# Where two of four RWKV pairs get their gates: behind the input projection, or between the levels of a triangular solve

## The chip, the cores and the metric

The kernel runs on one core of a Trainium2 chip. The metric is the device time of one launch in microseconds (us). Five engines work side by side and wait for each other by semaphores: TensorE (PE in the profile; PEld is its weight load), VectorE (DVE), ScalarE (ACT), GpSimd (POOL) and SyncE (SP), which here only issues DMAs. Each takes its instructions strictly in the order in which the program lists them.

## The reference, cut to what matters

One decoder layer for 512 prompt tokens and 8 sampled tokens (520 columns in all): a SwiGLU block, an input projection that feeds a differential-attention group and an RWKV-7 group, an output projection, and a second SwiGLU block. The change touches the RWKV part alone:

```
xm = prw + (prev - prw) * mu                      # token shift of the projected rows
r, k, v, xw, xa, xg = split(xm)                   # 512, 512, 512, 64, 64, 128 columns
w_log = -softplus(-(w0 + tanh(xw) @ w2)) - 0.5
decay = exp(-exp(w_log))                          # = exp(-exp(-0.5) * sigmoid(w0 + tanh(xw) @ w2))
a     = sigmoid(a0 + xa @ a2)
kk    = k * k_k;  kk = kk / max(sqrt(sum over a head of kk*kk), 1e-12)
k     = k * (1 + (a - 1) * k_a);   b = kk * a
# per head, over the tokens:  S = S * decay + (S @ -kk) b^T + v k^T ;  o = S @ r
```

The 8 RWKV heads of 64 are handled as 4 pairs of 128 rows (pairs 0 to 3). "Lora products" are `tanh(xw) @ w2` and `xa @ a2`; the two sigmoids of them are the decay gate and the rate gate.

## The kernel before

Everything lies feature-major: 128 partitions by 520 columns. The order of the whole program is written out by hand, one list of steps for each engine.

**Input projection** (`input_tensor`, `input_scalar`, `input_vector`, `input_pool`). 26 slabs j = 0..25, each one chunk of 128 output features, 48 matmuls. The order of chunks is RWKV's small columns (24, 25: tanh(xw) and xa, xg), the rotary chunks, then keys, r and v of the pairs and the attention values. Slabs from 4 on use accumulators 0 and 1 in turn; accumulator 2 is free for small products, and accumulator 3 takes the cache logits. Behind slab j (in order on TensorE) come the small steps: lora halves of pair 0 behind slabs 12 and 14, of pair 1 behind 18 and 20 (`half_lora_tensor`, two matmuls each), head sums of the squared keys behind 15 and 21 (`summed_tensor`), and from slab 10 on one group of cache pages each (`decode_keys_tensor`, 8 matmul records). ScalarE splits the next weights, drains the slab and does the gates; VectorE does the low halves of the split weights, the token shift and the exponents.

**Phase 0/1** then handles pairs 0 and 1 on the engines: an opening (`opening_tensor`, products and transposes of the features), five levels l = 0..4 that double the size of inverted blocks (`levels_tensor`, `levels_scalar`, `levels_vector`), a solve, and a state chain over n = 1..7 (`chain_tensor`, `chain_vector`). Within each level two ticks of attention are woven in (tick 2l + n): logits, maximum on VectorE, two exponentials with sums on ScalarE, a scaling, a transposition; and groups of cache pages. **Phase 2/3** does the same for the other pairs. Pairs 2 and 3 get their gates in phase 0/1: at level 0 (pair 2) and level 3 (pair 3) TensorE makes both lora products (`lora_tensor`, L964/L965), ScalarE the two sigmoids (`gates_scalar`, L1012/L1013) into the scratch rows LW and AG, the key factor and the squared keys (`factor_scalar`, L1022, L1024); at levels 1 and 4 TensorE sums the squares per head (L979), ScalarE takes the root (L1972), and VectorE the reciprocal behind level 1 and in the solve (`keys_inverse_vector`, L1075/L1076). VectorE's scans (L1057) and POOL's exponents and products follow, and POOL ends a pair with two copies into the step columns (L1121/L1122), on which the next pair's gates wait.

**PSUM ring.** The small products of the phases go through four banks in a fixed order (`ring_order`): a job may start when the jobs that held its banks have been read. The lora products are two jobs of two banks, that is the whole ring, and the key sums one job of one bank.

**State chain.** For every n, TensorE multiplies the states (L1844) and VectorE adds (L2272); step n + 1 waits for both. In phase 0/1 VectorE does after n = 4: `step_out_vector` (L2136, L2141), `decode_sums_vector` (seven small operations, L1387 to L1393) and `bonus_terms_vector` (L2147). TensorE's `decode_weights_tensor` (L1409) at n = 5 waits for the decode sums.

SP issues weight and page loads; the load of the third lora matrix (LG2, same space as LORA) waits for pair 3's rate product.

Of the kernel before, what the change touches and what calls it, by code (L numbers as in the profile page):

```python
# [112 lines left out]
def layer(nc, x_in, gu_a, down_a, w_in, w_out, gu_b, down_b, consts, vecs, lams, lora, g2,  # L113
# [15 lines left out]
    lo_dram = nc.dram_tensor("trunk_lo", (P, DC, TOK), f32, kind="Internal").ap()  # L129

    ctx = ExitStack()
    with ctx:
# [658 lines left out]
        def ring_order():  # L791
# [10 lines left out]
            for two, before, nxt in (((0, 1), (), (2, 3)), ((2, 3), (0, 1), ())):  # L802
# [14 lines left out]
                for l in range(N_LEVELS):  # L817
# [4 lines left out]
                    if nxt and l in (0, 3):  # L822
                        add(("decay", nxt[l // 3]), "s", 2)
                        add(("rate", nxt[l // 3]), "s", 2)
                    if nxt and l in (1, 4):
                        add(("keys", nxt[l // 4]), "s")
# [133 lines left out]
        def lora_tensor(pe, i, w, a):  # L960

            for n in range(2):
                cols = slice(HALF * n, HALF * n + HALF)
                m0 = nc.tensor.matmul(w[:, n, 0:HALF], LORA[0:64, i, :], PROJ[0:64, 24, cols], start=True, stop=True)  # L964
                m1 = nc.tensor.matmul(a[:, n, 0:HALF], LORA[64:P, i, :], PROJ[64:P, 24, cols], start=True, stop=True)  # L965
            return m0, m1
# [31 lines left out]

        def decay_gate_scalar(act, i):
            act.wait_ge(g("lora_done"), 2 * i + 1)  # L1000
            if i:
                act.wait_ge(g("step_columns"), i)
            nc.scalar.activation(halves(LW), accv(2), ACT.Sigmoid, bias=pv(i, 0)).then_inc(g("decay_read"), 1)

        def rate_gate_scalar(act, i):
            act.wait_ge(g("lora_done"), 2 * i + 2)
            nc.scalar.activation(halves(AG), accv(2), ACT.Sigmoid, bias=pv(i, 1)).then_inc(g("rate_read"), 1)

        def gates_scalar(act, i, w, a):

            act.wait_ge(g("step_columns"), i)
            nc.scalar.activation(halves(LW), w, ACT.Sigmoid, bias=pv(i, 0)).then_inc(g("bank_read_s"), 1)  # L1012
            nc.scalar.activation(halves(AG), a, ACT.Sigmoid, bias=pv(i, 1)).then_inc(g("bank_read_s"), 1)  # L1013

        def factor_scalar(act, i):
# [3 lines left out]
            else:  # L1019
                was_taken(act, ("rate", i))  # L1020
            act.wait_ge(g("vectors_set"), 1)
            nc.scalar.activation(FACTOR[:, :], AG, ACT.Identity, scale=pv(i, 3), bias=KEPT_KA[:, i:i + 1]).then_inc(g("gates"), 1)  # L1022
            was_shifted(act, 16 + i)
            nc.scalar.activation(KN, pj(16 + i), ACT.Square, scale=pv(i, 2)).then_inc(g("keys_squared"), 1)  # L1024
# [47 lines left out]
        def keys_inverse_vector(dve, i):  # L1072

            was_taken(dve, ("keys", i))
            dve_then(dve, nc.vector.tensor_scalar(KN[:, 0:HALF], KN[:, 0:HALF], 1e-12, None, ALU.max))  # L1075
# [159 lines left out]
        def input_scalar(act):  # L1235
            for j in range(N_IN):
# [22 lines left out]
                if j == 21:  # L1259
                    decode_own_scalar(act)  # L1260
# [1462 lines left out]
```

## Time and profile before

| | |
|---|---|
| three runs, us | 1325.09, 1330.69, 1326.98 (median 1326.98) |
| the profiled execution | 1320.13 us, its span 1318.3 us |
| granted TensorE clock, mean | 0.986 |
| PE busy | 1253.5 us (95%) |
| DVE busy | 558.8 us (42%) |
| ACT busy | 425.7 us (32%) |
| POOL busy | 109.1 us (8%) |
| chain that ended last | PE 84%, DVE 6%, ACT 3%, issue 2%, SPq 2%, DMA 1% |

Times inside the execution count from the start of its span. The first SwiGLU block ends at about 400 us, the input projection runs to 589 us, phase 0/1 to 735 us, phase 2/3 to 850 us, and the rest is output projection, second SwiGLU block and norms. A time in brackets in a timeline row is how long the engine was idle before the instruction and who released it. PEclk is the granted share of the full clock of 2.4 GHz: 0.50 is 1.2 GHz.

### The profile page before, as it was taken

How to read it: one execution, taken by the hardware profiler on the slowest of the kernel's cores; microseconds unless marked ns; L12 is line 12 of the kernel's file. 1: busy time of each engine (PE TensorE's matmuls, PEld its weight loads, DVE VectorE, ACT ScalarE, POOL GpSimd, SP SyncE). 2: the span in 40 equal slices, each digit the busy share in tenths (PEclk: the TensorE clock that was granted, in tenths of full speed). 3: DMA queues.
4: the chain of work that ended last, by engine and by line, in shares of the span. 5: the costliest groups of instructions: out<-in, count | busy, mean ns of one | idle time of the engine just before them, and what ended most of it. 6: DMA issues, size and time to landing. Idle time of an engine off the chain costs nothing.

```text
span 1318.3 us, 30092 instructions
## 1 busy us (share of the span) xinstructions
PE 1253.5 (95%) x12902; PEld 1132.4 (86%) x12902; DVE 558.8 (42%) x818; ACT 425.7 (32%) x657; POOL 109.1 (8%) x101
## 2 busy tenths in 40 slices
PE   9999999999998999997887999898999999999996
PEld 7999999999998988875446545697999999999995
DVE  4323332323436444253563554668533332322253
ACT  4222223221323324324553334323422222221222
POOL 0000000000110110000450012013000000000021
PEclk9999999999999999998998999999999999999999
DMA  6222222222223667544453799751222222222221
GB/s 226 96 95 92 75 88 95 68 89 88 88 86 112 260 198 248 193 154 146 157 165 119 246 312 313 251 186 35 94 96 95 95 95 93 67 79 88 89 65 66
DMA packets 56692, 174.79 MB, mean 133 GB/s; under 512 B 7185, under 2 KB 7442, under 8 KB 48274
## 3 DMA queue, kind: packets, MB, share of 16 engines
q1 hardware_dynamic: 54578, 169.48, 38.4%
q10 hardware_dynamic: 2016, 3.88, 0.8%
q8 instruction: 75, 1.23, 0.4%
q14 instruction: 23, 0.19, 0.0%
HBM read 163.58 MB, written 9.76 MB: 131 GB/s over the span
## 4 chain that ended last, share of the span: by engine, by line
PE 84%; DVE 6%; ACT 3%; issue 2%; SPq 2%; DMA 1%; POOL 0%; ACTq 0%; DVEq 0%
PE acc L295 66%; PE acc L318 5%; PE acc L1362 2%; SPq L2457 1%; PE acc L1432 1%; PE acc L971 1%; PE acc L1627 1%; PE acc L1619 1%; SPq L2449 1%; PE acc L1594 1%; PE acc L1604 1%; DVE weights_lo L278 1%; ACT map L1554 1%; PE acc L1510 1%; DMA y_sum<-in_x 1%
## 5 line engine op out<-in xcount | busy, mean ns | idle before, releaser
L278 DVE TENSOR_TENSOR weights_lo<-weights_raw,weights_hi 128x1024 fp32r<-128x1024 f32 (+2 forms) x184 | 208.4, 1134 | 533.4 <-ACT weights_hi L271 533.3
L271 ACT ACTIVATE weights_hi<-weights_raw 128x1024 fp32r<-128x1024 f32 (+2 forms) x184 | 177.5, 967 | 551.8 <-PE acc L295 520.8
L295 PE MATMUL acc<-x_hi,weights_hi 128*128 128x260 f32 x1696 | 344.2, 284 | 1.2 <-DVE weights_lo L263 1.2
L295 PE MATMUL acc<-x_hi,weights_lo 128*128 128x260 f32 x1696 | 341.7, 283 | 0.0
L295 PE MATMUL acc<-x_lo,weights_hi 128*128 128x260 f32 x1696 | 341.1, 283 | 0.0
L295 PEld LDWEIGHTS acc<-x_hi,weights_hi 128*128 128x128 f32 x1696 | 261.7, 188 | 14.3 <-issue 11.7
L295 PEld LDWEIGHTS acc<-x_hi,weights_lo 128*128 128x128 f32 x1696 | 261.4, 188 | 0.0
L295 PEld LDWEIGHTS acc<-x_lo,weights_hi 128*128 128x128 f32 x1696 | 260.7, 188 | 0.0
L295 PE MATMUL acc<-hidden_hi,weights_hi 128*128 128x260 f32 x704 | 143.1, 284 | 0.0
L295 PE MATMUL acc<-hidden_hi,weights_lo 128*128 128x260 f32 x704 | 141.7, 283 | 0.0
L295 PE MATMUL acc<-hidden_lo,weights_hi 128*128 128x260 f32 x704 | 141.6, 283 | 0.0
L295 PEld LDWEIGHTS acc<-hidden_hi,weights_hi 128*128 128x128 f32 x704 | 108.5, 188 | 1.7 <-issue 1.6
L295 PEld LDWEIGHTS acc<-hidden_lo,weights_hi 128*128 128x128 f32 x704 | 108.6, 188 | 0.0
L295 PEld LDWEIGHTS acc<-hidden_hi,weights_lo 128*128 128x128 f32 x704 | 108.6, 189 | 0.0
L593 POOL TENSOR_TENSOR scratch<-y_sum 128x520 f32<-128x520 f32 x3 | 4.8, 1613 | 664.2 <-DVE y_sum L372 664.2
L345 ACT ACTIVATE hidden_hi<-scratch 128x520 f32 (+1 forms) x44 | 28.1, 639 | 85.8 <-DVE scratch L355 85.8
L358 DVE TENSOR_TENSOR hidden_lo<-scratch,hidden_hi 128x520 f32 (+1 forms) x44 | 30.8, 701 | 38.9 <-ACT hidden_hi L345 38.9
L1362 PE MATMUL acc<-cache_pages,query_columns 128*32 128x512 f32 x256 | 35.8, 633 | 0.0
L318 PE MATMUL acc<-x_hi,weights_hi 128*128 128x260 f32 x128 | 26.5, 289 | 6.8 <-DVE x_lo L688 6.8
L1604 PEld LDWEIGHTS acc<-level_y,inverse_turned 64*64 64x64 f32 x768 | 13.8, 137 | 20.3 <-issue 16.9
L599 POOL TENSOR_TENSOR scratch<-scratch,y_sum 128x520 f32<-128x520 f32 x15 | 25.0, 1666 | 70.8 <-DVE y_sum L436 66.9
L355 DVE TENSOR_TENSOR scratch<-scratch,acc 128x520 f32<-128x520 f32 x44 | 30.3, 689 | 0.0
(337 smaller groups left out, 1338.3 us busy)
## 6 DMA issues: line engine op xcount, KB each, us to landing
cache_pages<-in_cache_k SPq DMA_DIRECT2D x128, 256.0 KB, 3.5
weights_raw<-in_gate_up_b SPq DMA_DIRECT2D x22, 1024.0 KB, 4.8
weights_raw<-in_gate_up_a SPq DMA_DIRECT2D x21, 1024.0 KB, 4.8
cache_pages<-in_cache_v SPq DMA_DIRECT2D x64, 256.0 KB, 3.7
weights_raw<-in_w_in SPq DMA_DIRECT2D x13, 1024.0 KB, 6.4
projected<-in_cache_v SPq DMA_DIRECT2D x48, 256.0 KB, 3.6
weights_raw<-in_down_a SPq DMA_DIRECT2D x8, 768.0 KB, 4.2
weights_raw<-in_down_b SPq DMA_DIRECT2D x8, 768.0 KB, 4.2
```

Of the source, the lines that this page charges most:

```text
L271: nc.scalar.activation(WH[pr.slot(k)][:, 0:nk, :], RAW[slot][:, 0:nk, P * (k % 2):P * (k % 2) + P], ACT.Copy).then_inc(split_hi, 1)
L278: nc.vector.tensor_tensor(WL[pr.slot(k)][:, 0:nk, :], RAW[slot][:, 0:nk, P * (k % 2):P * (k % 2) + P], WH[pr.slot(k)][:, 0:nk, :].bitcast( ...
L295: mm = nc.tensor.matmul(acc[s][:, a, 0:HALF], w[slot][:, t, :], x[:, k0 + t, HALF * a:HALF * a + HALF], start=begins and t == tiles[0] and ...
L318: mm = nc.tensor.matmul(acc[s][:, a, 0:HALF], w[slot][:, t, :], x[:, t, HALF * a:HALF * a + HALF], start=seen[k] == 1 and m == 0, stop=see ...
L345: nc.scalar.activation(HH[:, bass.ds(2 * (i - 1) + k - 2, 1), :], SCR[:, k:k + 1, :], ACT.Copy).then_inc(h_hi, 1)
L355: dve.tensor_tensor(halves(SCR[:, k, :]), halves(SCR[:, k - 2, :]), accv(k), ALU.mult).then_inc(hidden, 1)
L358: dve.tensor_tensor(HL[:, bass.ds(c, 1), :], SCR[:, k:k + 1, :], HH[:, bass.ds(c, 1), :].bitcast(f32), ALU.subtract).then_inc(acc_free[k], 1)
L599: pool.tensor_tensor(SCR[:, 5, :], Y[:, 0, :] if c == 1 else SCR[:, 5, :], Y[:, c, :], ALU.add)\
L971: mm = nc.tensor.matmul(out[:, n, 0:HALF], weights, x[:, HALF * n:HALF * n + HALF], start=True, stop=True)
L1362: mm = nc.tensor.matmul(bank(DECODE_BANK)[32 * h:32 * h + 32, :], QZ[:, h, b, :], PG[k % RING_GROUPS][:, :, P * h:P * h + P], start=b == 0 ...
L1432: mm = nc.tensor.matmul(bank(DECODE_BANK)[32 * j:32 * j + 8, :], WZ[:, n, 8 * b:8 * b + 8], page(N_GROUPS + k, j), start=False, stop=k == ...
L1604: mm = nc.tensor.matmul(two_banks(name)[64 * q:64 * q + 64, r, 64 * k:64 * k + 64], flat(lhs)[rows, cols], flat(rhs)[rows, cols], start=Tr ...
```

## The change

The lora halves of all four pairs are computed behind slabs 12, 13, 14, 16, 17, 18, 19 and 20 of the input projection, through accumulator 2. The gates of pairs 2 and 3 are put into rows 0, 1, 4, 5 of Y and written to a DRAM tensor by ScalarE's queue (behind slabs 15, 17, 18, 20); the squared keys of pairs 2 and 3 follow into rows 4 and 5, one folded sum behind slab 24, one root, and one reciprocal for both pairs at slab 25, kept in Y row 1. In levels 0 and 3 ScalarE issues two DMAs that bring the gates back into LW and AG and makes the key factor behind the exponentials of the level's first tick. The ring loses its lora and key jobs. In the state chain the decode sums (phase 0/1) and the bonus terms (both phases) move from n = 4 to n = 5 on VectorE. Decay gates of pairs 0 and 1 move one slab forward on ScalarE.

```diff
+        HALF_AT = {12: (0, 0), 13: (2, 0), 14: (0, 1), 16: (2, 1), 17: (3, 0), 18: (1, 0), 19: (3, 1), 20: (1, 1)}
+        HALF_ORDER = list(HALF_AT.values())
+        EARLY = [half for half in HALF_ORDER if half[0] >= 2]
+        EARLY_ROWS = (0, 1, 4, 5)
+        KEYS_INVERSE = Y[:, 1, 0:HALF]
+        def half_free(pe, j):
...
+            if j in (13, 19):
+                pe.wait_ge(g("decay_read"), j // 19 + 1)
+            if j in (14, 17, 18, 20):
+                pe.wait_ge(g("early_gates"), {14: 1, 17: 2, 18: 3, 20: 4}[j])
+            if j == 16:
+                pe.wait_ge(g("keys_normed"), 1)
+        def early_gate_scalar(act, half):
+            n = EARLY.index(half)
+            half_done(act, half)
+            act.wait_ge(g("roped"), 8)
+            nc.scalar.activation(halves(Y[:, EARLY_ROWS[n], :]), accv(2), ACT.Sigmoid, bias=pv(*half)).then_inc(g("early_gates"), 1)
+        def early_gate_out(act, n):
+            act.wait_ge(g("early_gates"), n + 1)
+            act.dma_start(gates_dram[n, :, :], Y[:, EARLY_ROWS[n], :]).then_inc(g("early_saved"), 16)
+        def early_squares_scalar(act, i):
+            act.wait_ge(g("early_saved"), 4 * 16)
+            was_shifted(act, 16 + i)
+            nc.scalar.activation(Y[:, 2 + i, :], pj(16 + i), ACT.Square, scale=pv(i, 2)).then_inc(g("early_squares"), 1)
+        def early_keys_tensor(pe):
+            pe.wait_ge(g("keys_normed"), 2)
+            pe.wait_ge(g("early_squares"), 2)
+            folded_tensor(acc[2][:, 0, :], (Y[:, 4, :], Y[:, 5, :])).then_inc(g("early_summed"), 1)
+        def early_keys_scalar(act):
+            act.wait_ge(g("early_summed"), 1)
+            nc.scalar.activation(KEYS_INVERSE, acc[2][:, 0, 0:HALF], ACT.Sqrt).then_inc(g("early_normed"), 1)
+        def early_keys_vector(dve):
+            dve.wait_ge(g("early_normed"), 1)
+            dve_then(dve, nc.vector.tensor_scalar(KEYS_INVERSE, KEYS_INVERSE, 1e-12, None, ALU.max))
+            nc.vector.reciprocal(KEYS_INVERSE, KEYS_INVERSE).then_inc(g("keys_inverse"), 1)
+        def gates_back(act, i):
+            act.wait_ge(g("step_columns"), i)
+            act.wait_ge(g("early_saved"), 4 * 16)
+            for n, x in enumerate((LW, AG)):
+                act.dma_start(x, gates_dram[2 * i - 4 + n, :, :]).then_inc(g("gates_back"), 16)
...
@@ input_scalar: per slab j
-                if j in (13, 19):
-                    decay_gate_scalar(act, j // 19)
+                if j in (12, 18):
+                    decay_gate_scalar(act, j // 18)
+                if j in (15, 17, 18, 20):
+                    early_gate_out(act, (15, 17, 18, 20).index(j))
+                if j in (13, 17, 19):
+                    early_gate_scalar(act, HALF_AT[j])
+                if j in (22, 23):
+                    early_squares_scalar(act, j - 20)
+                if j == 24:
+                    early_keys_scalar(act)
...
                 if j in (16, 22):
                     decays_scalar(act, j // 22)
+                if j == 16:
+                    early_gate_scalar(act, HALF_AT[j])
@@ input_vector
+                if j == 25:
+                    early_keys_vector(dve)
@@ levels_tensor
-                if nxt and l in (0, 3):
-                    i = nxt[l // 3]
-                    ring_free(pe, ("decay", i))
-                    ring_free(pe, ("rate", i))
-                    for mm in lora_tensor(pe, i, two_banks(("decay", i)), two_banks(("rate", i))):
-                        ring_full(mm)
-                if nxt and l in (1, 4):
...
-                    ring_full(folded_tensor(one(("keys", i)), (KN, KN)))
@@ levels_scalar
                 if nxt and l in (0, 3):
-                    i = nxt[l // 3]
-                    take(act, ("decay", i))
-                    take(act, ("rate", i))
-                    gates_scalar(act, i, wide(("decay", i)), wide(("rate", i)))
-                    factor_scalar(act, i)
-                if nxt and l in (1, 4):
...
-                    was_read(nc.scalar.activation(KN[:, 0:HALF], one(("keys", i))[:, 0:HALF], ACT.Sqrt), ("keys", i))
+                    gates_back(act, nxt[l // 3])
...
                 for n in range(2):
                     attention_exp_scalar(act, 2 * l + n, a, b)
+                    if nxt and l in (0, 3) and n == 0:
+                        factor_scalar(act, nxt[l // 3])
                     attention_turn_scalar(act, 2 * l + n, a, b)
@@ levels_vector, solve_vector
-                    if nxt and 2 * l + n == 3:
-                        keys_inverse_vector(dve, nxt[0])
...
-            if nxt:
-                keys_inverse_vector(dve, nxt[1])
@@ chain_vector
                 if n == 4:
                     step_out_vector(dve, b)
-                    if nxt:
-                        decode_sums_vector(dve)
-                    bonus_terms_vector(dve, b)
+                if nxt and n == 5:
+                    decode_sums_vector(dve)
                 if nxt and n >= 5:
                     for name in OPENED_AT[n]:
                         opened_vector(dve, name)
+                if n == 5:
+                    bonus_terms_vector(dve, b)
@@ sync, page group 28
-                    full(sp, ("rate", 3))
+                    sp.wait_ge(g("lora_done"), len(HALF_ORDER))
```

## Rows read from the trace of the kernel before

**Rows 1.** Windows, input projection: us, engines' busy, PEclk, DMA share, GB/s.
```profile
470.00:590.00 120.00, 119.06 (x985) 100.98 (x984) 52.40 (x107) 40.75 (x68) 5.85 (x8) 1.00 0.59 194
```

**Rows 2.** Chain of waits, a half product: start us, us, what.
```profile
490.09 1.07 PE acc L995 x4
```

**Rows 3.** Timeline of VectorE, opening of phase 0/1: start, duration, [idle before].
```profile
590.81 0.69 DVE L2152 TENSOR_TENSOR t_turned<-acc,constants 128x512 f32<-128x512 f32 x1 [0.88 <-PE acc L1594]
```

**Rows 4.** Timeline of TensorE, opening and level 0.
```profile
591.64 1.29 PE L1594 MATMUL acc<-features 64*64 64x64 f32 x64 [0.53 <-DVE t_turned L2152]
...
619.29 1.11 PE L1524 MATMUL acc<-projected 64*128 64x256 f32 x4 [2.26 <-ACT map L1554]
```

**Rows 5.** Timeline of ScalarE, level 0.
```profile
610.15 0.60 ACT L1920 ACTIVATE inverse_turned<-acc 128x512 f32<-128x512 f32 x1 [0.22 <-PE acc L1627]
...
613.07 1.28 ACT L1012 ACT_TABLE_LOAD   x1 [2.33 <-PE acc L965]
...
615.68 0.82 ACT L1022 ACTIVATE y_sum<-scratch,kept_key,feature_vectors 128x520 f32<-128x520 f32 x1
...
617.14 1.28 ACT L1554 ACT_TABLE_LOAD   x1
...
621.50 0.47 ACT L1554 ACTIVATE map<-acc,prompt_small 128x256 f32<-128x256 f32 x1 [1.37 <-DVE prompt_small L1568]
```

**Rows 6.** Timeline of VectorE, level 0: maximum of the first logits.
```profile
613.79 0.43 DVE L1568 TENSOR_REDUCE prompt_small<-acc 128x2 f32<-128x256 f32 x1 [4.34 <-PE acc L1527]
```

**Rows 7.** Windows of 2 us: TensorE's granted clock in stretches of 2 and 12 us.
```profile
618.00:620.00 2.00, 0.71 (x4) 0.39 (x4) 0.38 (x2) 1.99 (x7) 0.00 (x0) 0.86 0.81 237
...
640.00:642.00 2.00, 1.97 (x36) 1.88 (x37) 1.26 (x3) 0.00 (x0) 1.92 (x2) 0.50 0.05 12
...
694.00:696.00 2.00, 0.26 (x16) 0.12 (x8) 0.00 (x0) 0.00 (x0) 0.00 (x0) 1.00 0.68 201
...
715.00:727.00 12.00, 11.69 (x116) 9.52 (x119) 2.52 (x7) 1.42 (x3) 0.00 (x0) 0.50 0.12 43
```

**Rows 8.** Timeline of ScalarE, first exponentials of levels 1, 3 and 4.
```profile
630.62 0.58 ACT L1554 ACTIVATE map<-acc,prompt_small 128x384 f32<-128x384 f32 x1
...
661.06 0.47 ACT L1554 ACTIVATE map<-acc,prompt_small 128x256 f32<-128x256 f32 x1
...
670.69 0.58 ACT L1554 ACTIVATE map<-acc,prompt_small 128x384 f32<-128x384 f32 x1
```

**Rows 9.** Timeline of VectorE, levels 1 and 4.
```profile
628.60 0.96 DVE L1568 TENSOR_REDUCE prompt_small<-acc 128x2 f32<-128x768 f32 x1 [1.84 <-PE acc L1527]
...
636.97 1.78 DVE L1076 RECIPROCAL scratch<-scratch 128x260 f32<-128x260 f32 x1
...
668.67 0.96 DVE L1568 TENSOR_REDUCE prompt_small<-acc 128x2 f32<-128x768 f32 x1 [1.24 <-PE acc L1527]
```

**Rows 10.** Timeline of TensorE, level 1.
```profile
626.85 0.65 PE L979 MATMUL acc<-scratch,constants 128*32 128x260 f32 x8
...
640.03 1.13 PE L1604 MATMUL acc<-inverse,t_turned 64*64 64x64 f32 x32 [2.34 <-DVE value_blocks L2130]
```

**Rows 11.** Timeline of POOL: last copy of pair 2's features.
```profile
654.03 0.20 POOL L1122 COPY step_columns<-scratch 128x8 f32<-128x8 f32 x1
```

**Rows 12.** Landing times: tile decode_state, then the cache pages' issues.
```profile
DMA to landing us min/median/max: 2.0/5.8/11.0
...
cache_pages<-in_cache_k SPq DMA_DIRECT2D x128, 256.0 KB, 3.5
```

**Rows 13.** Timeline of VectorE, state chain at n = 4.
```profile
710.46 0.69 DVE L2141 TENSOR_REDUCE group_out<-value_blocks 128x8 f32<-128x512 f32 x1
...
713.27 0.47 DVE L2272 SCALAR_TENSOR_TENSOR state_added<-acc,gains,state_added 128x64 f32<-128x64 f32 x2
```

**Rows 14.** Timeline of TensorE, state chain at n = 5.
```profile
713.70 0.69 PE L1594 MATMUL acc<-features 64*64 64x64 f32 x32 [2.16 <-DVE state_added L2272]
...
714.32 3.06 PE L1409 MATMUL acc<-weight_columns,y_sum 128*128 128x64 f32 x16
```

More of the change, by code:

```diff
@@ L129, in layer @@
     lo_dram = nc.dram_tensor("trunk_lo", (P, DC, TOK), f32, kind="Internal").ap()
+    gates_dram = nc.dram_tensor("early_gates", (4, P, TOK), f32, kind="Internal").ap()
     ctx = ExitStack()
@@ L958, in layer @@
         KAPPA = math.exp(-0.5)
[L960 to L966, printed above, removed]
         def summed_tensor(out, weights, x):
@@ L997, in half_lora_tensor, with half_done @@
             mm.then_inc(g("lora_done"), 1)
+        HALF_AT = {12: (0, 0), 13: (2, 0), 14: (0, 1), 16: (2, 1), 17: (3, 0), 18: (1, 0), 19: (3, 1), 20: (1, 1)}
[3 more added lines that the diff above has]
+        KEYS_INVERSE = Y[:, 1, 0:HALF]
+        def half_done(eng, half):
+            eng.wait_ge(g("lora_done"), HALF_ORDER.index(half) + 1)
+        def half_free(pe, j):
+            if j == 12:
+                pe.wait_ge(g("rope_sin"), 8)
+                pe.wait_ge(g("lora_in"), 16)
+                pe.wait_ge(g("rates_in"), 1)
+            if j in (13, 19):
[4 more added lines that the diff above has]
+                pe.wait_ge(g("keys_normed"), 1)
@@ L1005, in rate_gate_scalar @@
         def rate_gate_scalar(act, i):
-            act.wait_ge(g("lora_done"), 2 * i + 2)
+            half_done(act, (i, 1))
             nc.scalar.activation(halves(AG), accv(2), ACT.Sigmoid, bias=pv(i, 1)).then_inc(g("rate_read"), 1)
[L1009 to L1013, printed above, removed]
         def factor_scalar(act, i):
@@ L1019, in factor_scalar @@
             else:
-                was_taken(act, ("rate", i))
+                act.wait_ge(g("gates_back"), 32 * (i - 1))
             act.wait_ge(g("vectors_set"), 1)
             nc.scalar.activation(FACTOR[:, :], AG, ACT.Identity, scale=pv(i, 3), bias=KEPT_KA[:, i:i + 1]).then_inc(g("gates"), 1)
-            was_shifted(act, 16 + i)
-            nc.scalar.activation(KN, pj(16 + i), ACT.Square, scale=pv(i, 2)).then_inc(g("keys_squared"), 1)
+            if i < 2:
+                was_shifted(act, 16 + i)
+                nc.scalar.activation(KN, pj(16 + i), ACT.Square, scale=pv(i, 2)).then_inc(g("keys_squared"), 1)
         def decays_scalar(act, i):
@@ L1963, in levels_scalar @@
                 if nxt and l in (0, 3):
-                    i = nxt[l // 3]
-                    take(act, ("decay", i))
-                    take(act, ("rate", i))
-                    gates_scalar(act, i, wide(("decay", i)), wide(("rate", i)))
-                    factor_scalar(act, i)
-                if nxt and l in (1, 4):
-                    i = nxt[l // 4]
-                    take(act, ("keys", i))
-                    was_read(nc.scalar.activation(KN[:, 0:HALF], one(("keys", i))[:, 0:HALF], ACT.Sqrt), ("keys", i))
+                    gates_back(act, nxt[l // 3])
                 if nxt and l == 2:
```

34 lines of the change are left out of this document (9 added, 25 removed).

## The prediction

> **What bounds the kernel now.** I read the windows first. In the input projection TensorE is busy 119.06 of 120 us at full clock, ScalarE 40.75 and VectorE 52.40 [rows 1]: whatever is put on TensorE there is paid in full, and the other two engines have room. The chain of waits says the same: it runs through TensorE's slabs and the small products behind them [rows 2]. In phase 0/1 that is no longer so. The chain there goes through ScalarE and VectorE, and TensorE stands idle for them: 2.26 us at level 0 until the first exponentials end [rows 4], 2.34 us at level 1 until VectorE has done its step products [rows 10], 2.16 us in the state chain at n = 5 [rows 14]. Third, the granted clock: after each of these three stalls it is lower, 0.86 on the way down, then 0.50 in the two other stretches (1.2 instead of 2.4 GHz), and at 0.50 it stays for 12 us behind the stall of the state chain [rows 7]. A stretch with TensorE nearly idle, 0.26 of 2 us, passed at 1.00 [rows 7]. So a stall costs itself and sometimes the work behind it once more.
>
> **Input projection, added: +4.9 us.** Four more lora halves stand behind slabs 13, 16, 17 and 19. One costs 1.07 us on the path [rows 2]: 4 x 1.07 = 4.3. The folded key sum behind slab 24 costs what such a sum costs in level 1, 0.65 us [rows 10]. Nothing hides them, TensorE being full [rows 1]. The new waits on TensorE (for the gate that last read accumulator 2) should all be met: each is asked one slab (some 7 us) after its gate could start. The tightest is behind slab 17: ScalarE must do split, drain, exponents of pair 0, then a table load of 1.28 us (as in [rows 5]) and the sigmoid; I estimate 6.8 us against 8 us. If it is missed, slab 18 waits about as much as it is late, and everything behind. Four DMA issues and two squares go onto ScalarE, four writes onto its DMA queue; ScalarE works a third of the time here [rows 1], so they are hidden. They stand ahead of nothing that TensorE asks for within a slab. SP's queue gains: its wait for pair 3's rate product becomes one that was met long ago; it was not what held the pages, I give it 0.
>
> **Opening, added: +1.2 us.** VectorE must do the maximum and the reciprocal for both pairs, 0.3 + 1.78 us [rows 9], behind the last token shift. It now has 0.88 us of idle time there [rows 3], and TensorE is released by the very next instruction [rows 4]. 2.1 - 0.9 = 1.2 us. Bounds 0 and 2.1.
>
> **Level 0: -4.5 us.** Before, the two lora jobs need the whole ring, so they wait for ScalarE's copies (the second starts at 610.15), and the sigmoid table is loaded at 613.07; sigmoids, factor and squares follow, then the exponential table at 617.14, and the first exponential can begin at 618.42 [rows 5]. The maximum that it really needs began at 613.79 [rows 6], and would come about 2.7 us earlier without the products, at 611.1. With 0.4 us for it and one table load left, the first exponential begins at about 612.9, some 5.5 us earlier. TensorE then finds its second logits ready when it comes to them, at about 614.5 instead of 619.29 [rows 4]: 4.8 earlier. On ScalarE the factor (0.82 us) follows and must wait until both gates have landed. The trace shows no reload of this kind; loads of 256 KB on ScalarE's queue took 2.0 to 11.0 us, pages of the same size 3.5 [rows 12]. I take 3.5, since the queue of pages is quiet then: issued by 611.7, landed at 615.2. The second exponential keeps its distance to the first (621.50 - 618.42 = 3.1 us) plus 0.8 for the factor and 1.4 for the landing, so about 618.2 instead of 621.50 [rows 5]. The level ends where TensorE and VectorE end it: I take -4.5. At a landing of 2.0 it is -4.8, at 6.0 about -2, at 11.0 about +2.6.
>
> **Level 1: -3.4 us.** The root and its two table loads go. The exponentials started at 630.62 [rows 8], though their maximum, begun at 628.60 for 0.96 us [rows 9], was there at 629.56; without the key sum (0.65 us, [rows 10]) ahead of the logits it is there at 628.9. 630.62 - 628.9 = 1.7. Then VectorE's reciprocal of 1.78 us [rows 9] goes from in front of the step products for which TensorE waited 2.34 us [rows 10]: 1.7, as they then wait for TensorE instead. Bounds -1.7 and -3.9.
>
> **Level 3: -1.5 us.** Here the order is less kind. The reload must wait for POOL's last copy of pair 2, at 654.03 [rows 11], issue until 655, land, and this level has no exponential in its first tick, so the factor comes at once and holds ScalarE until the landing: 658.3 at 3.5 us. Factor, one copy of 0.6, then the exponential at about 659.6 instead of 661.06 [rows 8]. At 2.0 it is -2.9, at 6.0 +1.0, at 11.0 +6.
>
> **Level 4: -1.6 us**, like the first half of level 1: 670.69 [rows 8] against a maximum ready at 668.67 + 0.96 - 0.65 = 669.0 [rows 9]. The reciprocal in the solve goes too; TensorE's own products end about when it did, so 0.
>
> **State chain: -1.1 us.** The sum over VectorE's step output ends at 711.15; only then come seven decode operations and the bonus terms, and the state at n = 5 at 713.27 [rows 13]. It will start at about 711.2. TensorE had its next product at 713.70 and the decode weights at 714.32 [rows 14]. The decode sums (1.6 us) now end at about 713.2, so the decode weights come 1.1 earlier. TensorE's one stall of 2.16 becomes two of under a microsecond. In phase 2/3 other products of TensorE fill the place: 0.
>
> Sum without the clock: 4.9 + 1.2 - 4.5 - 3.4 - 1.5 - 1.6 - 1.1 = -6.0 us.
>
> **The clock: -6.8 us.** Behind n = 5 twelve microseconds pass at 0.50 [rows 7]; the 16 products of the decode weights alone take 3.06 us [rows 14]. At full clock that stretch would be 6 us shorter at the most; two copies by ScalarE between the products don't scale, so I take 4.8. At levels 0 and 1 it is 1.0 each, for the two to four microseconds behind the stalls that go. Lower end 0, if the clock falls all the same; upper end 8.6.
>
> Together -12.8 us: 1320.13 - 12.8 = 1307.3 for an execution like the profiled one. That one lies 6.85 below the median of the runs, 1326.98; from the median it is 1314.2.
>
> The trace shows on ScalarE a table load of 1.28 us, and at 617.14 + 1.28 the exponentials begin with nothing between [rows 5]. The Trainium skill ("ScalarE: Activation LUTs", section "What ACT_TABLE_LOAD costs") gives the same load, and a drain of some 1.38 us with it, about 2.66 us a switch. By that rule the seven loads that go in the levels would bring up to 9.7 us more than by the load alone, and about 1304 instead of 1314 would come out. No row here shows the drain, so the rule gets 1 chance in 100.
>
> **Rivals.** First, the clock falls anyway. For it: the new opening gives TensorE a stall of about 1.7 us (0.53 + 1.2, [rows 4]) that could start a fall of its own, worth 3 to 4 us of work at half rate. Against it: 0.26 of 2 us busy passed at full clock [rows 7]. Then -6.0 stays, or -2 with the fall in the opening: 1321 to 1325; take 1322.
>
> Second, the slots freed are taken again: pages, POOL's products or instruction issue become what TensorE waits for, and phase 0/1 gives back what the levels gain, while the 4.9 and 1.2 stay. Pages land in 3.5 us [rows 12] and are asked for every 4 to 10 us, which speaks against. About 0: 1327.
>
> Third, slower: the reload is late. The page loads and the two reloads share the DMA engines; if the second gate lands 11.0 us after its issue, as the slowest load of this size on this queue [rows 12], level 0 is +2.6 and level 3 +6 instead of -4.5 and -1.5. Then 6.1 + 2.6 + 6.0 - 3.4 - 1.6 - 1.1 = +8.6, and with longer stalls no gain from the clock: 1336. It decides against the change from a landing of about 8 us on. For it: median 5.8 on that queue [rows 12]; against: those were issued next to other loads.
>
> **How the numbers follow.** The sum as it stands 0.51, the drain rule 0.01, the clock rival 0.25, given back 0.14, late reload 0.09. What a measurement of this kernel can tell from no change is about 0.5%, 6.6 us, here 1320.3. Faster: 0.51 + 0.01 + half of 0.25 = 0.65; same: the other half of 0.25, the 0.14 and a little of the last, 0.28; slower 0.07. The likeliest alone spans 1309 to 1319. The range for 8 in 10 is 1307 to 1327: it takes in the clock rival and most of the second, and leaves out the late reload.
>
> **What would show it.** In the changed profile: L995-like half products twice as many (8 calls, 1.07 us each) and slabs 13 to 20 back to back, PE at 99% of that window; VectorE's first masked copy about 1.2 us later behind the last token shift; one table load in levels 0 to 4 instead of eight; ScalarE's idle time before the factor 1 to 2 us at level 0 and about 3 at level 3, released by the DMA; TensorE's 2.26, 2.34 and 2.16 us stalls under 1 us, and the clock at 1.00 from n = 5 to the end of the chain. The prediction is wrong if the gates take over 6 us to land, if a half product's wait shows between slabs 16 and 20, or if the clock falls at n = 5 though the stall is gone.

## The result and the profile after

| | before | after |
|---|---|---|
| median of the runs, us | 1326.03 (1320.46 to 1330.69, 4 runs) | 1311.29 (1302.71 to 1312.62, 4 runs) |
| ratio | | 0.9897, 95% interval 0.9861 to 0.9933 |
| the profiled execution, us | 1320.13 (span 1318.3) | 1310.99 (span 1309.1) |
| granted TensorE clock, mean | 0.986 | 0.990 |
| ACT busy, us | 425.7 | 417.4 |

The change makes the kernel faster by 1.0%; 1314.2 was predicted. Two later executions, one of E1 and one of E4, ran at a mean clock of 0.85 and 0.65 (1387.9 and 1740.7 us) and are left out of every figure. I follow the profiled execution after the change through the same places as before. First the windows of the input projection (columns as in [rows 1]), then TensorE's timeline there: a half product of the new kind and the next one.

```profile
470.00:590.00 120.00, 120.00 (x976) 101.13 (x975) 51.98 (x103) 44.64 (x73) 5.84 (x8) 1.00 0.58 197
```
```profile
498.62 1.14 PE L986 MATMUL acc<-projected,lora_weights 64*128 64x260 f32 x4
506.63 1.14 PE L986 MATMUL acc<-projected,lora_weights 64*128 64x260 f32 x4
```

TensorE has no idle time at all, so no new wait shows between the slabs, and a slab with its small product repeats every 8.01 us. The projection ends at 594.38 instead of 589.02 us. Of these 5.36 us, 0.6 are there before slab 12.

The opening, VectorE and then TensorE (against [rows 3] and the first of [rows 4]):

```profile
595.21 0.29 DVE L1039 TENSOR_SCALAR y_sum<-y_sum 128x260 f32<-128x260 f32 x1
595.53 1.78 DVE L1040 RECIPROCAL y_sum<-y_sum 128x260 f32<-128x260 f32 x1
597.23 0.63 DVE L2184 TENSOR_TENSOR t_turned<-acc,constants 128x512 f32<-128x512 f32 x1
```
```profile
598.00 1.29 PE L1642 MATMUL acc<-features 64*64 64x64 f32 x64 [1.52 <-DVE t_turned L2184]
...
655.75 0.45 PE L1553 MATMUL acc<-constants,map 128*128 128x128 f32 x1 [2.69 <-issue]
...
705.02 0.69 PE L1642 MATMUL acc<-features 64*64 64x64 f32 x32 [0.37 <-ACT scratch L1958]
706.66 2.00 PE L1457 MATMUL acc<-weight_columns,y_sum 128*128 128x64 f32 x16 [0.94 <-DVE own_weights L1441]
```

The reciprocal stands in front of VectorE's first masked copy, and TensorE's stall grows from 0.53 to 1.52 us. The last two rows are the state chain at n = 5: the 2.16 us of [rows 14] have become 0.37 and 0.94, and the 16 decode products take 2.00 us at full clock instead of 3.06.

ScalarE in levels 0 and 3 (against [rows 5] and [rows 8]):

```profile
616.17 0.60 ACT L1958 ACTIVATE inverse_turned<-acc 128x512 f32<-128x512 f32 x1 [9.47 <-PE acc L1675]
...
617.08 0.82 ACTq L1047 DMA_DIRECT2D scratch<-early_gates  x2
617.93 1.28 ACT L1602 ACT_TABLE_LOAD   x1 [0.31 <-issue]
619.23 0.37 ACT L1602 ACTIVATE map<-acc,prompt_small 128x128 f32<-128x128 f32 x1
...
620.55 0.82 ACT L1066 ACTIVATE y_sum<-scratch,kept_key,feature_vectors 128x520 f32<-128x520 f32 x1 [0.51 <-DMA scratch<-early_gates]
...
623.23 0.47 ACT L1602 ACTIVATE map<-acc,prompt_small 128x256 f32<-128x256 f32 x1 [1.09 <-DVE prompt_small L1616]
...
626.77 1.09 ACT L1958 ACTIVATE inverse_turned<-acc 128x512 f32<-128x512 f32 x2 [1.53 <-PE acc L1675]
...
649.55 0.83 ACTq L1047 DMA_DIRECT2D scratch<-early_gates  x2
654.35 0.82 ACT L1066 ACTIVATE y_sum<-scratch,kept_key,feature_vectors 128x520 f32<-128x520 f32 x1 [5.28 <-DMA scratch<-early_gates]
655.08 0.57 ACT L1585 ACTIVATE values_turned<-acc 128x512 f32<-128x512 f32 x1
655.56 0.46 ACT L1602 ACTIVATE map<-acc,prompt_small 128x256 f32<-128x256 f32 x1
```

From ScalarE's first copy of level 0 to that of level 1 it is 10.6 us (616.17 to 626.77) instead of 17.2. The copy at 610.15 in [rows 5] is the second one of that level. This is the first, in the profile of before; the first of level 1 starts at 626.52 there:

```profile
609.34 0.60 ACT L1920 ACTIVATE inverse_turned<-acc 128x512 f32<-128x512 f32 x1 [8.99 <-PE acc L1627]
```

At level 3 the factor holds ScalarE for 5.28 us, and the copy for which TensorE waits stands behind it: it ends at 655.65, and TensorE goes on at 655.75 after 2.69 us. The view calls that stall "issue", yet it ends with the copy, and in E7 below, where the copy stands ahead of the factor, the same products run without it.

The windows with the granted clock (third column from the end), against [rows 7]:

```profile
614.00:616.00 2.00, 1.91 (x31) 1.79 (x32) 0.69 (x1) 0.00 (x0) 0.00 (x0) 0.57 0.03 8
...
640.00:642.00 2.00, 2.00 (x52) 1.33 (x52) 1.20 (x2) 1.65 (x7) 0.55 (x2) 1.00 0.30 97
654.00:656.00 2.00, 0.25 (x2) 0.28 (x2) 0.00 (x0) 1.65 (x4) 0.00 (x0) 0.81 1.05 399
656.00:658.00 2.00, 2.00 (x7) 0.49 (x10) 1.16 (x7) 1.24 (x6) 0.00 (x0) 0.50 0.98 361
...
705.00:717.00 12.00, 10.28 (x259) 8.89 (x261) 7.19 (x20) 1.42 (x3) 0.00 (x0) 1.00 0.15 52
...
734.00:736.00 2.00, 1.89 (x12) 0.34 (x10) 1.46 (x3) 1.40 (x4) 0.00 (x0) 0.50 1.05 376
908.00:910.00 2.00, 2.00 (x11) 2.00 (x11) 1.54 (x3) 1.46 (x2) 0.00 (x0) 0.50 0.03 8
```

The clock holds over the state chain (705 to 717), which was the largest single hope. It falls at level 0, behind a wait of TensorE of 1.49 us of kind "issue" (614 to 618), behind level 3's new stall, once in phase 2/3, and once at the start of the second SwiGLU block, which it does not do in the profile of before.

Before, level 0 had more of it than [rows 7] show. The clock is already down from 608 to 616 us, behind a wait of 1.69 us of the same kind, and the lora products run at half rate (here a window of the profile of before):

```profile
612.00:614.00 2.00, 2.00 (x16) 1.33 (x16) 0.21 (x1) 0.93 (x1) 0.00 (x0) 0.50 0.00 0
```

Last, TensorE's waits for cache pages in phase 2/3:

```profile
775.31 1.04 PE L1480 MATMUL acc<-cache_pages,query_columns 128*8 128x512 f32 x8 [0.36 <-DMA cache_pages<-in_cache_v]
778.52 1.04 PE L1480 MATMUL acc<-projected,query_columns 128*8 128x512 f32 x8 [1.28 <-DMA projected<-in_cache_v]
...
790.42 1.04 PE L1480 MATMUL acc<-cache_pages,query_columns 128*8 128x512 f32 x8 [0.65 <-DMA cache_pages<-in_cache_v]
793.01 1.04 PE L1480 MATMUL acc<-projected,query_columns 128*8 128x512 f32 x8 [0.43 <-DMA projected<-in_cache_v]
```

They add up to 2.72 us; before there were two, 0.49 and 0.67. The bill by places, each stage from its start to the next in the two profiled executions: input +5.4; opening +1.0; from there to level 0 +0.5; levels 0 to 4: -6.6, -4.5, -0.6, -0.4, -1.6; solve and chain up to the decode weights -0.9; from there to the values -5.6 (half rate before, full rate after); phase 2/3 +2.8; the rest +1.3 (the clock at 908). Together -9.2, as the spans differ. The last term is not the change's: of the fourteen profiled executions of this study all but those of the kernel before and of E1 have a fall at that place, with the old gates (E5, E9, E11) as with the new.

### The profile page after: what moved, and what is told of

Its sections match the earlier page's. It is cut to its first block, busy times and chain, and to the rows that moved or that the text cites. A ratio compares the mean times of both kernels' runs of the same rounds, so it can differ in the third digit from the quotient of the medians.

```text
span 1309.1 us, 30080 instructions
## 1 busy us (share of the span) xinstructions
PE 1250.0 (95%) x12894; PEld 1131.0 (86%) x12894; DVE 557.1 (43%) x816; ACT 417.4 (32%) x650; POOL 109.0 (8%) x101
## 4 chain that ended last, share of the span: by engine, by line
PE 87%; DVE 6%; issue 2%; ACT 2%; SPq 2%; DMA 1%; POOL 0%; ACTq 0%; DVEq 0%; POOLq 0%
PE acc L296 66%; PE acc L319 5%; PE acc L1410 2%; PE acc L1480 2%; PE acc L962 1%; PE acc L1675 1%; SPq L2487 1%; PE acc L1652 1%; PE acc L1667 1%; DVE weights_lo L279 1%; PE acc L1755 1%; PE acc L986 1%; PE acc L2649 1%; SPq L2479 1%; PE acc L1558 1%
## 5 line engine op out<-in xcount | busy, mean ns | idle before, releaser
L296 PEld LDWEIGHTS acc<-x_hi,weights_hi 128*128 128x128 f32 x1696 | 261.8, 188 | 12.8 <-issue 11.7
L1652 PEld LDWEIGHTS acc<-level_y,inverse_turned 64*64 64x64 f32 x768 | 13.8, 137 | 18.3 <-issue 15.7
```

The costliest lines, as they stand in the source:

```text
L296: mm = nc.tensor.matmul(acc[s][:, a, 0:HALF], w[slot][:, t, :], x[:, k0 + t, HALF * a:HALF * a + HALF], start=begins and t == tiles[0] and ...
L1652: mm = nc.tensor.matmul(two_banks(name)[64 * q:64 * q + 64, r, 64 * k:64 * k + 64], flat(lhs)[rows, cols], flat(rhs)[rows, cols], start=Tr ...
```

## How far single times can be read

Runs of one kernel lie up to 18 us apart (before: 1315.5 to 1333.6 in 69 runs beside those of the experiments). Most of it goes with the clock. A line through 165 runs of all kernels, with one slope and one constant for each kernel, gives 1053 us (+/- 45) per unit of (1 - mean granted clock) and leaves a scatter of 1.9 us. The constant is a kernel's time at a mean clock of 1.00. A constant is an extrapolation, but it parts "does less" from "keeps the clock better". E7 and E8, with one run each, are not in the table.

| kernel | runs | mean us | mean clock | constant, us |
|---|---|---|---|---|
| before | 69 | 1325.0 | 0.9840 | 1308.2 |
| after (E3 included) | 12 | 1312.8 | 0.9887 | 1300.8 |
| E1 chain order only | 11 | 1323.0 | 0.9845 | 1306.6 |
| E2 gates only | 12 | 1317.7 | 0.9852 | 1302.2 |
| E4 both late | 9 | 1312.1 | 0.9877 | 1299.1 |
| E5 before, filled | 12 | 1321.9 | 0.9879 | 1309.2 |
| E6 after, filled | 6 | 1314.1 | 0.9883 | 1301.9 |
| E9 before, half values | 10 | 1317.1 | 0.9869 | 1303.3 |
| E10 after, half values | 4 | 1308.8 | 0.9872 | 1295.4 |
| E11 no switch | 12 | 1318.5 | 0.9838 | 1301.3 |
| E12 both late, filled | 6 | 1311.0 | 0.9905 | 1301.0 |

One constant is good to about 1.9 us over the root of its number of runs: 0.6 for twelve, 1.0 for four; differences are taken before rounding. The change is -7.3 us (+/- 0.6) at full clock and -4.9 us (+/- 1.3, from the scatter of the mean clocks) by the clock (0.0047 x 1053). The prediction had -6.0 and -6.8.

## The experiments

**E1, E2, E3, E4** were timed side by side, with the kernel before among them.

E1: the kernel before with the new order of the chain only (E2: the kernel after with the old order).

```diff
                 if n == 4:
                     step_out_vector(dve, b)
-                    if nxt:
-                        decode_sums_vector(dve)
-                    bonus_terms_vector(dve, b)
+                if nxt and n == 5:
+                    decode_sums_vector(dve)
...
+                if n == 5:
+                    bonus_terms_vector(dve, b)
```

> The kernel before with VectorE's new order in the state chain alone. Theory A (stall and clock): TensorE's stall at n = 5 goes from 2.16 us to under 1 us, the decode weights start 0.9 to 1.1 us earlier, and the 12 us behind them, at a granted clock of 0.50 before, pass at 1.00, which is worth some 5.5 us more: 6.0 to 6.7 us in all, ratio 0.995. Theory B (stall alone; the clock in the changed kernel stayed up because TensorE had been busier in the levels before): about 1 us, ratio 0.999, and the clock falls here as it did.

Measured: 1322.93 us, ratio 0.9988 (0.9965 to 1.001). The stall is cut as in the kernel after, but the clock falls all the same. TensorE's timeline at n = 5, and the window behind:

```profile
710.54 0.69 PE L1594 MATMUL acc<-features 64*64 64x64 f32 x32 [0.37 <-ACT scratch L1920]
712.18 2.00 PE L1409 MATMUL acc<-weight_columns,y_sum 128*128 128x64 f32 x16 [0.95 <-DVE own_weights L1393]
715.28 3.67 PE L1409 MATMUL acc<-weight_columns,y_sum 128*128 128x64 f32 x16
```
```profile
712.00:724.00 12.00, 11.51 (x140) 9.39 (x144) 3.75 (x9) 1.42 (x3) 0.00 (x0) 0.60 0.15 51
```

The first 16 products run in 2.00 us, the second 16 at half rate in 3.67. So the order alone is worth its 1.1 us (constant -1.5) and almost nothing in clock (0.0005, that is 0.5 us +/- 0.9).

> The changed kernel with VectorE's old order in the state chain. Theory A: TensorE's stall of 2.2 us at n = 5 is back and the clock falls to 0.50 behind it; the kernel is 6 to 7 us slower than the changed one, that is 6 to 8 us faster than the one before, ratio 0.994 to 0.995. Theory B: the clock stays up, 1 us slower than the changed kernel, ratio 0.990.

Measured: 1318.11 us, ratio 0.9941 (0.9912 to 0.997). The stall of 2.17 us is back and the clock over 706 to 718 us is 0.53. The gates' part of the change brings 6.0 us at full clock and 1.3 by the clock. Put on top of the gates (from E2 to the kernel after) the new order brings 3.6 us by the clock, alone (E1) it brought 0.5. The two differ by 3.1 us +/- 2.0, so E1's theory B, that the levels ahead matter for the clock at the chain, is neither shown nor excluded.

E3 is the kernel after once more.

> The changed kernel as it is, timed beside the others on one chip. Both theories: 13 to 14 us faster than before, ratio 0.9897 as measured (0.986 to 0.993).

Measured: 1315.17 us, ratio 0.9907 (0.9874 to 0.994). Its profiled execution took 1318.92 us with the same two short stalls. TensorE at n = 5, then the window:

```profile
708.16 0.69 PE L1642 MATMUL acc<-features 64*64 64x64 f32 x32 [0.37 <-ACT scratch L1958]
709.81 2.58 PE L1457 MATMUL acc<-weight_columns,y_sum 128*128 128x64 f32 x16 [0.95 <-DVE own_weights L1441]
```
```profile
710.00:724.00 14.00, 13.63 (x182) 11.31 (x183) 4.28 (x10) 1.42 (x3) 0.00 (x0) 0.54 0.13 44
```

The same kernel with the same stalls kept the clock in one profiled execution and lost it in the other. Whether the clock falls behind the short stalls is therefore a matter of the execution, not settled by the change. The counts over all profiles stand at the end of this section.

E4: the kernel after with pair 3's factor behind tick 7's exponentials and the key reciprocal behind level 0's first products.

```diff
-                    if nxt and l in (0, 3) and n == 0:
+                    if nxt and 2 * l + n in (0, 7):
                         factor_scalar(act, nxt[l // 3])
...
-                if j == 25:
-                    early_keys_vector(dve)
...
+                if nxt and l == 0:
+                    early_keys_vector(dve)
```

> The changed kernel with pair 3's key factor behind the exponentials of tick 7 instead of ahead of them, and the maximum and reciprocal of the key norms behind level 0's first products on VectorE instead of in front of the opening. Theory A (ScalarE's wait of 5.28 us for the reload at level 3 stands on the path, and so does VectorE's reciprocal in the opening): level 3 gains 2 to 3 us and the clock does not dip behind it, the opening gains 1.0; of these 3 to 4 us the page loads of phase 2/3 take up to 1: 2.5 to 4 us faster than the changed kernel, ratio 0.987. Rival (the level is then held by VectorE's scan, which needs the same factor): under 1.5 us in all, ratio 0.989.

Measured: 1312.53 us, ratio 0.9909 (0.9883 to 0.9935); constant 1.7 us (+/- 0.8) below the kernel after, between what the two theories say, but no lower time that could be told apart, since its mean clock was 0.001 lower.

**E5, E6, E7, E8** came next. E5: the kernel before with two products that nobody reads, 128x512, inside the stall of 2.16 us. E6: the kernel after with one ahead of the decode weights.

```diff
+                if nxt and n == 5:
+                    pe.wait_ge(g("exped"), 16)
+                    for _ in range(2):
+                        nc.tensor.matmul(bank(4), MEAN[:, :], CONST[:, 0:512], start=True, stop=True)
                 if nxt:
                     for name in OPENED_AT[n]:
                         opened_tensor(pe, name)
```

> The kernel before, VectorE's order untouched, with two idle products of 128x512 (about 0.86 us each) put on TensorE into the stall of 2.16 us at n = 5; they go to a bank that nobody reads. Theory A (the stall makes the clock fall): the decode weights start when they did, the 12 us behind them run at 1.00, 4 to 6 us faster, ratio 0.996, mean clock up by 0.004. Theory B (the clock falls behind this stretch by the thin work of the whole chain, whatever fills this one stall): no change, ratio 1.000, clock as before.

Measured: 1321.81 us, ratio 0.9977 (0.9956 to 0.9998). TensorE's timeline:

```profile
709.10 1.99 PE L1854 MATMUL acc<-constants,mean_weights 128*128 128x512 f32 x4
711.33 0.69 PE L1594 MATMUL acc<-features 64*64 64x64 f32 x32 [0.24 <-DVE state_added L2276]
711.95 2.00 PE L1409 MATMUL acc<-weight_columns,y_sum 128*128 128x64 f32 x16
```

The decode products run at full rate, and the mean clock rises by 0.0039 (4.1 us +/- 1.0), at a price of 1.0 in the constant; the net gain, 3.1 us in the mean, is under the 4 to 6 of theory A. Nothing but the idle time was changed, so the stall is shown to be what costs the clock there.

> The changed kernel with one idle product of 0.86 us in the 0.95 us that TensorE still waits for the decode sums. Theory A: the clock no longer falls behind n = 5 in any execution; mean clock up by up to 0.003 and 1 to 3 us faster than the changed kernel, ratio 0.988. Theory B: as the changed kernel, ratio 0.990, and a profile can show the fall all the same.

Measured: 1314.28 us, ratio 0.9914 (0.9881 to 0.9947). No fall at the chain, but no gain (theory B): constant +1.0, mean clock 0.9883, and TensorE waits 4.23 us for pages in its profile instead of 2.72.

E7 and E8 are the two halves of E4's edit, one profiled execution each.

> The changed kernel with pair 3's key factor behind the exponentials of tick 7. Theory A: ScalarE's exponentials at level 3 no longer wait for the reload, level 3 is 1.5 to 2.5 us shorter, and TensorE's 2.7 us stall in it is under 1.5 us. Rival: VectorE's scan waits in its place and the level keeps its length within 0.7 us.

Measured: 1316.87 us once. Level 3 takes 11.4 instead of 13.4 us, between TensorE's transposes. The wait has moved to VectorE, whose scan stands in front of what TensorE needs. ScalarE, VectorE, TensorE:

```profile
655.95 0.82 ACT L1066 ACTIVATE y_sum<-scratch,kept_key,feature_vectors 128x520 f32<-128x520 f32 x1 [1.14 <-DMA scratch<-early_gates]
...
656.81 0.84 DVE L1102 TENSOR_TENSOR_SCAN scratch<-constants,scratch 128x64 f32<-128x64 f32 x4 [1.08 <-ACT y_sum L1066]
...
658.37 0.69 PE L1652 MATMUL acc<-inverse,t_turned 64*64 64x64 f32 x32 [1.98 <-DVE value_blocks L2168]
```

The reload was issued from 651.13 on, so even here it was there only 4.8 us later. Behind the 1.98 us the clock falls here too (660 to 664 us).

> The changed kernel with the reciprocal of the key norms behind level 0's first products on VectorE. Theory A: TensorE's idle time between the opening's first and second products is 0.5 us again instead of 1.5, the opening is 1.0 us shorter and nothing is later in level 0. Rival: level 0's first maximum waits for the reciprocal in its place, and 0.5 us or more comes back there.

Measured: 1313.29 us once. The opening is back to a stall of 0.53 us (1.0 less), and level 0 does not grow (10.8 us between TensorE's transposes, 11.1 in the kernel after): the reciprocal had a free place there.

**E9 to E12** came last. E9 and E10 load half of each value page, in the kernel before and after.

```diff
-                    sp.dma_start(page(k, n), cache[bass.ds(pid, 1), :, :].rearrange("a p n -> (a p) n"))\
+                    half = slice(0, 512 if k < N_GROUPS else 256)
+                    sp.dma_start(page(k, n)[:, half], cache[bass.ds(pid, 1), :, half].rearrange("a p n -> (a p) n"))\
```

> The kernel before, with only half of the columns of each page of values loaded (the other half of each page keeps what was there; left out of the result). It asks whether the pages hold phases 2 and 3. In the profiled kernel before, TensorE waited 1.16 us in all for pages, after the change 2.72 us. Theory: the work ahead of the pages was the bound before, so this gains little: page waits to 0, 1.2 us less at full clock, up to 2 with what follows. Rival: pages bound nothing in either kernel (their waits cover others): within 0.5 us. A second rival: TensorE's clock stays up more often without the page waits, which would give 2 to 4 us besides.

Measured: 1316.67 us, ratio 0.9943 (0.9915 to 0.9971); constant -4.8 against the kernel before, more than either side expected.

> The kernel after with the same halving of the page loads. Theory: some 2.7 us less than the kernel after at full clock (1300.7 to about 1298), 1.5 us more than the same halving brings the kernel before, because the levels end 7 us earlier while the pages arrive at their own pace: that is what the change gives back in phase 2. Rival: the same small gain as on the kernel before (within 0.5 us of it), so that nothing is given back to pages.

Measured: 1308.87 us, ratio to the kernel before 0.9874 (0.983 to 0.9917); constant -5.4 against the kernel after. The difference between the two gains, 0.6 with an uncertainty of about 1.3, settles nothing between 1.5 and 0. The profiles say more. I summed TensorE's waits between 580 and 880 us that are for pages or of kind "issue", without level 3's stall (2.69 us after, 2.60 with half values), which belongs to ScalarE's copy: before 1.2 + 8.6 = 9.8 us, with half values 1.4 + 6.2 = 7.6; after 2.7 + 9.2 = 11.9, with half values 0.9 + 6.1 = 7.0. So halving takes 2.2 us of waits from the one and 4.9 from the other. The issue waits go with the page traffic: with whole pages they are 8.1 to 12.2 us in twelve profiles, with half values 6.2 and 6.1. That the levels give part of their gain back to the page traffic is not shown: the sum is 11.9 us in one execution of the kernel after and 10.1 in E3's of the same kernel, and 9.8, 9.8, 11.6 and 13.5 in the four with whole pages and the old gates (before, E11, E1, E5).

E11: the kernel before with sigmoids and roots of pairs 2 and 3 as scaled copies.

```diff
-            nc.scalar.activation(halves(LW), w, ACT.Sigmoid, bias=pv(i, 0)).then_inc(g("bank_read_s"), 1)
+            nc.scalar.activation(halves(LW), w, ACT.Copy, scale=0.01).then_inc(g("bank_read_s"), 1)
... (the rate gate and the root of the key norms likewise)
```

> The kernel before, in which the sigmoids of the gates of pairs 2 and 3 and the roots of their key norms are plain scaled copies on ScalarE (the values are not the reference's), so that all eight table loads in the levels go, while every product, transfer and reciprocal stays. It asks how much of the change's gain the loads alone would bring. Theory: each load costs its own 1.28 us where ScalarE is on the path (two at level 0, one or two at levels 1, 3, 4): 6 to 9 us less at full clock (1308.1 to about 1300), and perhaps some clock besides. Rival by the drain that the Trainium skill's page ScalarE: Activation LUTs adds to a load: eight times 2.66 us, up to 17 to 21 us less. Second rival: TensorE's lora products and VectorE's ring hold these levels, so less than 4 us.

Measured: 1319.29 us, ratio 0.9954 (0.9926 to 0.9983); constant -6.8, mean clock unchanged (0.9838). ScalarE in level 0:

```profile
611.38 0.60 ACT L1012 ACTIVATE scratch<-acc 128x520 f32<-128x520 f32 x1 [1.39 <-PE acc L965]
...
613.24 0.71 ACT L1024 ACTIVATE scratch<-projected,feature_vectors 128x520 f32<-128x520 f32 x1
613.86 0.35 ACT L1554 ACTIVATE map<-acc,prompt_small 128x128 f32<-128x128 f32 x1
```

Level 0 falls from 17.2 to 11.5 us (between ScalarE's first copies, clock included), with the products, the ring and the factor still in it. About half of these 5.7 us is the loads: from the first sigmoid's load, or the copy in its place, on to the first exponential it is 5.36 us before (613.07 to 618.43) and 2.48 here (611.38 to 613.86), 2.9 less, of which 0.2 are the copies' own shorter time. The other 2.8 lie where TensorE ran at half rate before and at full rate here: the eight lora products take 2.1 us in the one and 1.2 in the other. The eight loads of 1.28 us are 10.2 us in all, of which at most 6.8 lay on the path. This is about as much as the whole move of the gates brings net (6.0); the move also pays 4.8 us for the products in the input projection and 1.0 in the opening.

E12: E4's kernel with E6's idle product.

> The kernel after with three edits: pair 3's factor behind tick 7's exponentials, the key reciprocals behind level 0's first products, and one idle 128x512 product ahead of the chain's decode weights, which the stall there hides. Theory: 2 to 3 us less than after at full clock (1300.7 to about 1298, as the first two edits gave 1299.0 together) and no fall of the clock behind the chain in most executions, so a mean clock of 0.989 or more: ratio to before 0.986 to 0.989. Rival: the idle product delays the weights and the clock falls elsewhere instead: ratio 0.990 to 0.992, no better than the kernel after.

Measured: 1310.98 us, ratio 0.99 (0.9867 to 0.9934). The mean clock is the best of all (0.9905), and from the end of the input to the decode weights it needs 110.8 us against 113.3. Then TensorE in phase 2/3:

```profile
771.64 1.04 PE L1478 MATMUL acc<-cache_pages,query_columns 128*8 128x512 f32 x8 [0.52 <-DMA cache_pages<-in_cache_v]
776.73 1.18 PE L1478 MATMUL acc<-projected,query_columns 128*8 128x512 f32 x8 [3.16 <-DMA projected<-in_cache_v]
```

One page comes 3.16 us late, and from the values to the output projection it is 131.9 us instead of 126.9. No version with the right values beats the kernel after by more than can be measured.

Taken together, the profiled executions of all kernels show how often the clock falls behind n = 5, in the decode products:

| TensorE's stalls there | profiled executions | with a fall |
|---|---|---|
| one of 2.16 or 2.17 us | before, E2, E9, E11 | 4 of 4 |
| 0.37 and 0.95 us | after, E1, E3, E4, E7, E8, E10 | 3 of 7 (E1, E3, E10) |
| filled | E5, E6, E12 | 0 of 3 |

In the same profiles the clock falls behind level 3 in all nine executions with the reload (also with the factor late), and in one of the five without it; and in the opening in three of the six with the reciprocal ahead of it (E3, E6, E7), in none of the other eight.

## Why the prediction was right

- **Input +4.9.** Right: 4.8 once the 0.6 us from ahead of slab 12 are taken off. The worry about the wait behind slab 17 did not come true.
- **Opening +1.2.** Measured +1.0; E8 shows that it is the reciprocal. It was avoidable.
- **Level 0 -4.5.** With the clock -5.5 predicted, -6.6 measured. The parts were less exact: one table load stayed as predicted, the reload landed in time for 0.51 us of waiting instead of 1.4, and the first exponential came 3.1 us behind ScalarE's first copy instead of 9.1. The prediction took the fall behind the 2.26 us alone; the one from 608 to 616 us it did not see, so part of what it gave to the order of work was the clock's. How much differs by execution: between TensorE's transposes level 0 takes 17.2 us in the profile of before and 15.7, 16.3 and 16.3 in those of E1, E5 and E9, 11.1 in that of after and 10.1 in E4's, which has no fall there. The bounds are also off by a little: from a landing of 3.5 us to one of 11.0 the sum adds 7.5, which makes +3.0 and not +2.6; no run came near.
- **Level 1 -3.4.** With its clock -4.4 predicted, -4.5 measured; TensorE's wait of 2.34 us is 0.38.
- **Level 3 -1.5.** Measured -0.4, the fixed term whose working failed. The landing was taken as 3.5 us behind the issues; the factor started 4.8 us behind the first (649.55, factor at 654.35) and 4.4 behind the second, the longest landing of a gate in the profile. And I had looked at the exponentials only, not at the copy for TensorE behind the factor, whose delay made a stall of 2.69 us and a fall of the clock. E7: without that the level is 2.0 us shorter.
- **Level 4 -1.6.** Measured -1.6.
- **State chain -1.1.** Measured -0.9, and -1.5 (+/- 0.6) as E1's constant.
- **The clock -6.8.** The term that was mis-sized, if any was: -4.9 (+/- 1.3) in the mean of the runs. The stall causes the fall (E5), but behind the two short stalls that are left the clock still falls in some executions (3 of 7 profiles). At 5.6 us a fall, as in the pair of profiles, that is some 2.4 us by my estimate, enough for the difference. The sign that the prediction gave of being wrong, a fall at n = 5 though the stall is cut, is in E3's profile. The first rival, given 0.25, is thus true for a part of the executions, and the new stalls of the opening and of level 3 add falls of their own. The short stretch of 0.26 busy at 1.00, which I held against this rival, was no warrant.
- **Given back** (second rival): not the whole gain, and not shown to be a part of it. In the pair of profiles there are 1.6 us more page waits and 0.5 us more issue waits (level 3's stall taken out), but E3's profile of the same kernel has 1.14 us of page waits, as many as before (1.16). **Late reload** (third rival): 3.5 and 4.8 us after the issue, never near 8.
- **The drain rule.** At level 0 the load begins at 617.93, lasts 1.28 and the exponential starts at 619.23, and with eight loads gone E11 gains 6.8 us, less than the loads' own 10.2. In E11's level 0, where both loads stood in ScalarE's chain, they were worth 2.7 us together. The Trainium skill ("ScalarE: Activation LUTs", section "What ACT_TABLE_LOAD costs") would have them cost 2.66 us each; the measurement decides against that here.

The fixed part came out 1.3 us better (-7.3 against -6.0) and the clock 1.9 worse, so that the sum, -12.3 by the means of all runs against -12.8, is closer than its terms. That is luck. The pair of profiled executions, for which -12.8 was also said, differs by 9.1 us only (1320.13 and 1310.99).

## What to carry to other kernels

Read a stall twice: for its length, and for the granted clock behind it; to prove the second, fill the stall with a product that nobody reads and change nothing else. A shortened stall is not a removed one, so count the clock it would give back by a chance, not in full. When a step is put behind a transfer on an in-order engine, look at every instruction that stands behind it, above all at the copies for the bottleneck engine, not only at the step's own consumer.

## What the runs showed of the hardware

- The same kernel kept 1.00 or fell to 0.54 in the same place behind the same stalls of 0.37 and 0.95 us, in two executions; over all kernels with these stalls it fell in 3 of 7 profiles, behind one stall of 2.16 us in 4 of 4, with the stall filled in 0 of 3.
- Nearly all of the spread between executions of one kernel follows the mean granted clock: 1053 us per unit, 1.9 us left over.
- Halving the value pages (16.8 MB less read of 163.6 before, 164.6 after) shortened TensorE's waits of kind "issue" from 8.6 to 6.2 us before and from 9.2 to 6.1 after (level 3's stall taken out); in twelve profiles with whole pages they are never under 8.1. What these waits are, and why they go with the traffic, was not tried.
- A reload of two gates from DRAM on ScalarE's queue was there 3.5 us after the first issue at level 0 and 4.8 us at level 3, where the 2 us window in which it landed (654 to 656) shows a DMA share of 1.05.
